# A two-layer decoder step on one core: last down panels kept on chip, first panels of the next head loaded earlier, ScalarE's splits ahead of its squares, one boundary's squares summed by TensorE

## The chip, the cores and the metric

The kernel runs on one NeuronCore of one Trainium2 chip. The metric is the time of one execution on the device in microseconds (us). Engines are called TensorE (PE, with PEld for its weight loads), VectorE (DVE), ScalarE (ACT), GpSimd (POOL) and SyncE (SP, whose queue of transfers is SPq).

## What is computed

One step of a hybrid decoder with two layers over 1056 columns (a prompt of 1024 tokens and 8 x 4 sample tokens), model width 1024, FFN width 2816, everything in float32 accuracy. Layer 0 mixes a short convolution with differential attention, layer 1 is an mLSTM with four heads. Each sub-layer stands between two norms:

```python
h = h + rmsnorm(mix, g[1])
h = h + rmsnorm(swiglu(rmsnorm(h, g[2]), w_gu[layer], w_down[layer]), g[3])
# swiglu: (silu(x @ gate) * (x @ up)) @ w_down
```

## The kernel before

All activations lie transposed on chip: 128 partitions by (feature tile, 1056 columns), and the columns are worked on in three thirds of 352. A matrix product in near float32 accuracy is made of three float16 matmuls: weight and activation are each split in a high part and a low part, and high x high, high x low and low x high are accumulated. A weight panel is 128 output features by all input tiles (8 tiles for most, KF = 11 for w_down). It is called a *visit*. SyncE loads it raw to one of two buffers (`w_raw[:, v % 2]`, `load_tile`), and only when the low split of visit v-2 is done. ScalarE makes the high part (`split_hi`, L242), VectorE the low part (`split_lo`, L255), in one of three slots of `w_split`, or in a named row of `arena` (`home`). `split_at` says at which *unit* both engines make the split of a visit: at the first unit after the last one that used the same slot (or later, by `late`). A unit is one panel times one third: 8 x 3 = 24 or 11 x 3 = 33 matmuls at L282 into one of six PSUM banks, then an evacuation.

The order on every engine is written out by hand, as the generators that `woven` and `steps` interleave. Each engine runs its list strictly in order, and so a wait holds back all that is behind it.

A *boundary* is the end of a sub-layer: for each third g, eight units whose result y goes to `ybuf` (a *pass*, `PASS[b][g]`), then the chain of norms for this third, which is woven into the eight units of the next one:

- the sum of y's squares: ScalarE squares each of the eight tiles (`act_square`, L530), GpSimd adds them up (`pool_sums`, L538 and L541), TensorE multiplies by ones (`pe_sum`, L506) after unit 0 of the next third;
- the first root (ScalarE L552, L555, VectorE L580, L581), then h += y scaled, in four pairs of tiles (VectorE L597, L601);
- the squares of h (ScalarE L562), which TensorE adds up itself: eight matmuls with 32 columns of ones each (`pe_part_sums`, L516, after unit 3), a copy by ScalarE (L565, semaphore `part_made`) and a last matmul with ones (`pe_whole_sum`, L523, in the middle of unit 4);
- the second root and the new activation u, high and low (VectorE L613 and L586, ScalarE L571).

Boundary 0 is the end of layer 0's mixer (w_out, eight resident panels), boundary 1 the end of its FFN, boundary 2 the end of the mLSTM, whose passes are short (2 tiles, L699 adds the rest), boundary 3 the end of the second FFN and of the kernel. The FFN has two halves of 11 gate and 11 up panels. The first half's down product is made with each panel used for all three thirds; the second half's is the pass of boundary 1 or 3 (`add_last_down`), which goes third by third and so loads all eight panels three times. Among the loads of its last third in boundary 1 stand the first two panels of the mLSTM (`early_q`, columns of w_in1). After a boundary the next stage begins with twelve units of four panels, third by third (`WAVE`, `pe_wave`). In boundary 1 h is saved to memory by GpSimd's queue (`h_spill`), a third at a time.

## Time and profile before

| | us |
|---|---|
| runs, median (lowest to highest) | 2910.95 (2905.79 to 2916.68), 3 runs |
| profiled execution, its own time | 2908.74 |
| its span, first to last instruction | 2907.1 |
| TensorE, VectorE, ScalarE, GpSimd busy | 2766.8, 1106.4, 913.2, 246.0 |
| mean granted clock of TensorE | 0.983 |

An idle time in the profile stands ahead of an instruction, with the engine, tile and line that ended it. Matmuls overlap, so that one of 128x352 is shown with 313 ns while one starts about every 150 ns. A granted clock of 1 is 2.4 GHz, 0.5 is 1.2 GHz; for a stretch the mean is given.

### The profile page before, as it was taken

How to read it: one execution, taken by the hardware profiler on the slowest of the kernel's cores; microseconds unless marked ns; L12 is line 12 of the kernel's file. 1: busy time of each engine (PE TensorE's matmuls, PEld its weight loads, DVE VectorE, ACT ScalarE, POOL GpSimd, SP SyncE). 2: the span in 40 equal slices, each digit the busy share in tenths (PEclk: the TensorE clock that was granted, in tenths of full speed). 3: DMA queues.
4: the chain of work that ended last, by engine and by line, in shares of the span. 5: the costliest groups of instructions: out<-in, count | busy, mean ns of one | idle time of the engine just before them, and what ended most of it. 6: DMA issues, size and time to landing. Idle time of an engine off the chain costs nothing.

```text
span 2907.1 us, 46616 instructions
## 1 busy us (share of the span) xinstructions
PE 2766.8 (95%) x19289; PEld 1815.3 (62%) x19289; DVE 1106.4 (38%) x1880; ACT 913.2 (31%) x1703; POOL 246.0 (8%) x356
## 2 busy tenths in 40 slices
PE   6999899989999999999799999999979999999997
PEld 4666565656666666666467666667646666666665
DVE  4455542327322112225653434344473221122354
ACT  4444432225322112224333232324353221122232
POOL 3000013212000000001100001010220000000011
PEclk8999999999999999999999999999999999999998
DMA  5211269661112111124564323321401121111243
GB/s 193 76 59 39 71 209 331 232 215 37 36 45 60 51 44 44 51 62 120 115 84 59 66 55 69 59 71 58 150 1 47 48 62 48 43 45 52 65 140 110
DMA packets 297789, 248.60 MB, mean 86 GB/s; under 512 B 10900, under 2 KB 263162, under 8 KB 296940
## 3 DMA queue, kind: packets, MB, share of 16 engines
q1 hardware_dynamic: 278332, 172.53, 22.8%
q0 software_dynamic: 19248, 73.10, 7.2%
q8 instruction: 155, 2.54, 0.4%
q14 instruction: 54, 0.44, 0.0%
HBM read 218.77 MB, written 26.81 MB: 84 GB/s over the span
## 4 chain that ended last, share of the span: by engine, by line
PE 84%; DVE 7%; ACT 3%; issue 3%; DMA 2%; SPq 1%; POOL 0%; DVEq 0%; POOLq 0%; ACTq 0%
PE ps L282 68%; PE ps L1462 2%; DVE arena L597 1%; DMA w_raw<-in_w_in 1%; PE ps L1450 1%; DVE hT L601 1%; PE ps L1148 1%; PE ps L2028 1%; PE ps L2019 1%; PE ps L1227 1%; PE ps L1997 1%; DMA hT<-in_cache_v 1%; PE ps L1972 1%; PE ps L2011 1%; ACT w_split L242 1%
## 5 line engine op out<-in xcount | busy, mean ns | idle before, releaser
L282 PE MATMUL ps<-u,w_split 128*128 128x352 f16 x9936 | 1531.8, 314 | 11.4 <-DVE arena L1112 3.9
L282 PEld LDWEIGHTS ps<-u,w_split 128*128 128x128 f16 x9936 | 969.7, 98 | 533.6 <-issue 26.5
L282 PE MATMUL ps<-arena,w_split 128*128 128x352 f16 x3960 | 610.5, 315 | 9.3 <-DVE w_split L255 7.8
L255 DVE SCALAR_TENSOR_TENSOR w_split<-w_raw,w_split 128x1024 f16<-128x1024 f32 (+2 forms) x214 | 285.3, 1334 | 774.1 <-ACT w_split L242 773.7
L282 PEld LDWEIGHTS ps<-arena,w_split 128*128 128x128 f16 x3960 | 388.2, 98 | 226.8 <-issue 11.8
L242 ACT ACTIVATE w_split<-w_raw 128x1024 f16<-128x1024 f32 (+2 forms) x214 | 242.7, 1135 | 63.4 <-PE ps L282 45.8
L828 ACT ACTIVATE arena<-arena 128x352 f16<-128x352 f32 x132 | 65.6, 497 | 378.2 <-DVE arena L861 378.2
L834 ACT ACTIVATE arena<-ps 128x352 f32<-128x352 f32 x132 | 61.0, 462 | 316.0 <-PE ps L282 316.0
L861 DVE SCALAR_TENSOR_TENSOR arena<-ps,arena 128x352 f32<-128x352 f32 x132 | 69.2, 524 | 198.9 <-PE ps L282 197.9
L538 POOL TENSOR_TENSOR arena<-arena 128x352 f32<-128x352 f32 x12 | 13.0, 1084 | 1324.3 <-ACT arena L530 1314.4
L848 DVE TENSOR_TENSOR arena<-arena 128x352 f16<-128x352 f32 x132 | 69.3, 525 | 71.8 <-ACT arena L828 71.8
L530 ACT ACTIVATE arena<-arena 128x352 f32<-128x352 f32 x96 | 47.5, 496 | 148.9 <-DVE arena L663 141.6
L541 POOL TENSOR_TENSOR arena<-arena 128x352 f32<-128x352 f32 x72 | 73.3, 1019 | 231.4 <-ACT arena L530 230.1
L1841 ACT ACTIVATE arena<-ps 128x352 f32<-128x352 f32 x66 | 30.5, 463 | 193.2 <-PE ps L282 193.2
L836 ACT ACTIVATE arena<-ps 128x352 f32<-128x352 f32 x48 | 22.2, 463 | 193.9 <-PE ps L282 193.9
L282 PE MATMUL ps<-u,arena 128*128 128x352 f16 x504 | 78.6, 316 | 1.9 <-ACT arena L834 1.3
L1462 PE MATMUL ps<-ident,hT 128*128 128x128 f32 x512 | 69.6, 279 | 2.2 <-issue 1.9
L1462 PEld LDWEIGHTS ps<-ident,hT 128*128 128x128 f32 x512 | 55.5, 140 | 25.4 <-issue 24.9
L282 PEld LDWEIGHTS ps<-u,arena 128*128 128x128 f16 x504 | 49.3, 99 | 32.0 <-issue 5.9
L1591 DVE COPY arena<-ps 128x512 f32<-128x512 f32 x64 | 44.2, 691 | 60.2 <-PE ps L1462 59.8
L1300 DVE TENSOR_REDUCE small<-ps 128x1 f32<-128x128 f32 (+7 forms) x64 | 45.5, 752 | 42.9 <-PE ps L1151 42.9
L1531 ACT ACTIVATE arena<-ps 128x512 f32<-128x512 f32 x64 | 38.2, 597 | 72.2 <-PE ps L1462 72.2
(357 smaller groups left out, 2198.2 us busy)
## 6 DMA issues: line engine op xcount, KB each, us to landing
w_raw<-in_w_gu SPq DMA_DIRECT2D x88, 512.0 KB, 3.8
w_raw<-in_w_down SPq DMA_DIRECT2D x64, 704.0 KB, 4.6
w_raw<-in_w_in SPq DMA_DIRECT2D x56, 512.0 KB, 6.7
hT<-in_cache_k SPq DMA_DIRECT2D x64, 256.0 KB, 4.0
hT<-in_cache_k POOLq DMA_DIRECT2D x64, 256.0 KB, 4.3
hT<-in_cache_v SPq DMA_DIRECT2D x64, 256.0 KB, 4.9
hT<-in_cache_v POOLq DMA_DIRECT2D x64, 256.0 KB, 5.5
hT<-in_state_C POOLq DMA_DIRECT2D x32, 256.0 KB, 4.1
```

The costliest lines, as they stand in the source:

```text
L242: act.activation(split_of(v, 0)[:, 0:kt * n], w_raw[:, v % 2, 0:kt * n], ACT.Copy, scale=WS).then_inc(w_hi, 1)
L255: dve.scalar_tensor_tensor(split_of(v, 1)[:, 0:kt * n], w_raw[:, v % 2, 0:kt * n], WS, split_of(v, 0)[:, 0:kt * n], ALU.mult, ALU.subtract ...
L282: ins = pe.matmul(ps[0:m, bank, 0:GW], split_of(v, wp)[:, k * w + col * P:k * w + col * P + m], x[:, xp, k0 + k, cols(g)], start=(k == 0 a ...
L530: act.activation(sq_y[k % 2], ybuf[:, k, cols(gg % 3)], ACT.Square).then_inc(sq_ready, 1)
L541: pool.tensor_tensor(sum_y, sum_y, sq_y[k % 2], ALU.add).then_inc(y_added, 1)
L828: act.activation(hid[:, 0, i, cols(g)], hidf[:, cols(g)], ACT.Copy).then_inc(hid_hi, 1)
L834: act.activation(gate[:, cols(g)], ps[:, bank, 0:GW], ACT.Silu, scale=1 / WS).then_inc(evac["act"], 1)
L848: dve.tensor_tensor(hid[:, 1, i, c], hidf[:, c], hid[:, 0, i, c], ALU.subtract).then_inc(hid_ready, 1)
L861: dve.scalar_tensor_tensor(hidf[:, cols(g)], ps[:, UNITS[n].bank, 0:GW], 1 / WS, gate[:, cols(g)], ALU.mult, ALU.mult).then_inc(evac["dve" ...
L1300: dve.tensor_reduce(neg_mx[:, n % 4:n % 4 + 1], score_cols(i, c)[:, 0:(i + 1) * P], AX.X, ALU.max, negate=True).then_inc(nm_ready, 1)
L1462: ins = pe.transpose(ps[:, 4 + e, h * P:(h + 1) * P], ring[:, f % RING, h * P:(h + 1) * P], ident[:, :])
L1591: dve.tensor_copy(kt[n % 2][:, :, P:2 * P], ps[:, 5, :].rearrange("p (h e) -> p h e", h=HEADS)).then_inc(kp_ev[1], 1)
```

## The change

- In the last down passes (boundaries 1 and 3) panel 4, in boundary 3 panel 6 too, is loaded and split once, to `arena` rows 21 and 22 (26 and 27), and used by all three thirds. Rows 21 and 22 are the FFN's `hidf` and `gate`, so ScalarE waits there for the last up unit.
- The two first mLSTM panels are loaded in the second half of layer 0's FFN, after panels 4 and 7.
- In the passes ScalarE makes the high split that is due at unit n+1 already in the step of unit n, ahead of its wait for the drained unit and of the square. VectorE's order of low splits is as before.
- In boundary 0 the sums of h's squares come a unit later (`SUM_AT`), and the chain's steps are moved with them (`PASS_ACT[0]`, `PASS_DVE[0]`).
- In boundary 2 the squares of y go to eight places (`y_sq`), TensorE adds them up as it does those of h, ScalarE copies the result (`part_made`), `pe_sum` follows. GpSimd has no part in it. ScalarE's and VectorE's orders are rewritten; the first FFN panel's split is due at unit 0 of the last third, and no step of the FFN's wave comes before the end of the third chain's second root on ScalarE.

```diff
@@ split_of
+            if VISITS[v].kt == KF:
+                return rows(home, 2).rearrange("p a t -> p (a t)").bitcast(F16)[:, part_ * KF * P:(part_ + 1) * KF * P]
@@ splits_hi
-            for v in split_at.get(n, ()):
+            for v in hi_at.pop(n, ()):
                 split_hi(act, v)
@@ add_ffn(layer, b, wave, early=())
+                    if half_ and i in (4, 7):
+                        for add in early[i == 7:][:1]:
+                            add()
@@ add_last_down
-                    v = add_visit(p_cols(w_down[layer, KF * P:2 * KF * P, :], i), KF, ("last", layer, g, i))
-                    PASS[b][g].append(add_unit(v, "dve", g))
-                    if g == 2 and i in (5, 6):
-                        early(i - 5)
+                    if i not in stays:
+                        v = add_visit(p_cols(w_down[layer, KF * P:2 * KF * P, :], i), KF, ("last", layer, g, i),
+                                      home=kept.get(i))
+                        if i in kept:
+                            stays[i] = v
+                    PASS[b][g].append(add_unit(stays.get(i, v), "dve", g))
...
+        add_last_down(0, 1, {4: 21})
...
-        late[wave[0] + 1] = WAVE[2][8]
-        add_last_down(1, 3, lambda j: None)
+        late[wave[0]], late[wave[0] + 1] = PASS[2][2][0], WAVE[2][8]
+        add_last_down(1, 3, {4: 21, 6: 26})
...
+        hi_at = dict(split_at)
@@ pe_sum, pe_part_sums, act_square, act_chain (boundary 2)
+            if (0, gg) in PART_TURN:
+                pe.wait_ge(part_made, PART_TURN[0, gg] + 1)
...
-                ins = pe.matmul(ps[q:q + 32, 7, 0:GW], ones[:, 0:32], ybuf[:, k, cols(gg % 3)], start=(k < 4),
-                                stop=(k >= 4))
+                ins = pe.matmul(ps[q:q + 32, 6 + a, 0:GW], ones[:, 0:32], ybuf[:, k, cols(gg % 3)] if a else y_sq[k],
+                                start=(k < 4), stop=(k >= 4))
...
+            if b == 2:
+                act.wait_ge(h_part, PART_TURN[0, gg] + 1)
+                act.wait_ge(y_summed, gg)
+                act.activation(sum_y, ps[:, 6, 0:GW], ACT.Copy, scale=1 / 32).then_inc(part_made, 1)
+                yield
@@ orders of the passes
-        PASS_ACT = (2, 2, 1, 2, 1, 1, 1, 1)
-        PASS_DVE = (3, 2, 0, 0, 2, 1, 1, 1)
+        PASS_ACT = ((2, 2, 1, 0, 1, 2, 2, 1), (2, 2, 1, 2, 1, 1, 1, 1))
+        PASS_DVE = ((3, 2, 0, 0, 0, 2, 2, 1), (3, 2, 0, 0, 2, 1, 1, 1))
+        SUM_AT = (4, 3)
@@ act_last_units
+                if b % 2 and (g, i) == (0, 0):
+                    act.wait_ge(hid_ready, up_turn[up_unit[b // 2, 1, KF - 1, 2]] + 1)
+                splits_hi(act, n + 1)
                 drained(act, n)
                 act_square(act, 3 * b + g, i)
@@ pe_short_passes
-                    if (g, i) == (1, 1):
+                    if (g, i) == (1, 0):
+                        pe_part_sums(pe, 6, 0)
+                    if (g, i) == (1, 2):
                         pe_sum(pe, 6)
                     if (g, i) == (2, 0):
+                        pe_part_sums(pe, 7, 0)
+                    if (g, i) == (2, 1):
                         pe_sum(pe, 7)
-                    if (g, i) == (2, 1):
+                    if (g, i) == (2, 2):
                         pe_part_sums(pe, 6)
-                    if (g, i) == (2, 2):
+                    if (g, i) == (2, 4):
                         pe_whole_sum(pe, 6)
+            pe_part_sums(pe, 8, 0)
             pe_sum(pe, 8)
```

The end of ScalarE's order in boundary 2 (a, b, c are the chains of the three thirds; a chain's steps are now copy, first root, four squares, copy, second root, four of u):

```diff
             steps(units_[2], 2)
             steps(a, 2)
             steps(b, 2)
-            steps(c, 1)
+            steps(c, 2)
             steps(b, 2)
             steps(c, 2)
             steps(b, 4)
-            steps(wave, 4)
             steps(c, 4)
-            woven(wave, c, (1,) * 4 + (0,) * 4)
+            woven(wave, c, (1,) * 4 + (0,) * 8)
```

## Rows read from the trace of the kernel before

**Rows 1.** the page, busy time and share of the span, TensorE

```profile
PE 2766.8 (95%) x19289; PEld 1815.3 (62%) x19289; DVE 1106.4 (38%) x1880; ACT 913.2 (31%) x1703; POOL 246.0 (8%) x356
```

**Rows 2.** waits of TensorE over the whole span: total, times, longest

```profile
PE ps L506 <- POOL arena L541: 12.9, 5, 5.6
```

**Rows 3.** stages: length; PE, PEld, DVE, ACT, POOL busy; PE clock; DMA share; GB/s

```profile
1350.00:1510.00 160.00, 136.68 (x873) 83.39 (x871) 94.85 (x124) 63.32 (x88) 19.48 (x18) 0.95 0.53 106
1453.00:1460.40 7.40, 7.30 (x34) 4.01 (x35) 5.42 (x11) 2.72 (x5) 3.13 (x2) 0.68 0.84 87
2095.00:2205.00 110.00, 91.94 (x551) 53.95 (x549) 75.99 (x109) 56.67 (x100) 22.07 (x21) 0.94 0.07 21
```

**Rows 4.** timeline, boundary 1, last third: start, duration, what, idle before

```profile
1419.98 0.37 SPq L216 DMA_DIRECT2D w_raw<-in_w_in  x1
...
1429.27 1.06 ACT L242 ACTIVATE arena<-w_raw 128x1024 f16<-128x1024 f32 x1 [6.40 <-DMA w_raw<-in_w_in]
...
1432.95 1.54 PE L523 MATMUL ps<-arena,ones 128*128 128x352 f32 x2 [8.17 <-ACT arena L565]
...
1434.28 14.15 PE L282 MATMUL ps<-arena,w_split 128*128 128x352 f16 x84
...
1453.10 7.34 PE L282 MATMUL ps<-arena,w_split 128*128 128x352 f16 x33 [4.67 <-DVE w_split L255]
...
1466.29 0.83 PE L506 MATMUL ps<-arena,ones 128*128 128x352 f32 x2 [2.16 <-POOL arena L541]
```

**Rows 5.** timeline, boundary 1, second third

```profile
1369.23 1.63 DVE L255 SCALAR_TENSOR_TENSOR w_split<-w_raw,w_split 128x1408 f16<-128x1408 f32 x1 [0.16 <-ACT w_split L242]
...
1372.55 0.79 PE L516 MATMUL ps<-arena,ones 128*32 128x352 f32 x4 [2.02 <-ACT arena L562]
...
1376.79 0.86 PE L523 MATMUL ps<-arena,ones 128*128 128x352 f32 x2 [1.11 <-ACT arena L565]
```

**Rows 6.** DMA issues, KB each, us to landing: whole span; last row 1515 to 1700

```profile
w_raw<-in_w_gu SPq DMA_DIRECT2D x88, 512.0 KB, 3.8
w_raw<-in_w_down SPq DMA_DIRECT2D x64, 704.0 KB, 4.6
...
w_raw<-in_w_in SPq DMA_DIRECT2D x12, 512.0 KB, 7.0
```

**Rows 7.** timeline, boundary 0, last third

```profile
698.69 0.79 PE L516 MATMUL ps<-arena,ones 128*32 128x352 f32 x4 [1.72 <-ACT arena L562]
...
701.21 0.76 PE L523 MATMUL ps<-arena,ones 128*128 128x352 f32 x2
...
705.22 1.06 ACT L242 ACTIVATE w_split<-w_raw 128x1024 f16<-128x1024 f32 x1 [1.11 <-DMA w_raw<-in_w_gu]
```

**Rows 8.** timeline, boundary 2, sums, squares and chains

```profile
2126.70 1.39 PE L516 MATMUL ps<-arena,ones 128*32 128x352 f32 x16
...
2133.94 0.52 DVE L580 SCALAR_TENSOR_TENSOR arena<-ps,arena 128x352 f32<-128x352 f32 x1
...
2143.43 1.51 PE L506 MATMUL ps<-arena,ones 128*128 128x352 f32 x2 [5.56 <-POOL arena L541]
...
2145.82 0.58 DVE L597 SCALAR_TENSOR_TENSOR arena<-arena,gains 128x352 f32<-128x352 f32 x1
...
2149.90 0.79 ACT L562 ACTIVATE arena<-hT 128x704 f32<-128x704 f32 x1 [1.25 <-DVE hT L601]
...
2156.97 0.52 DVE L580 SCALAR_TENSOR_TENSOR arena<-ps,arena 128x352 f32<-128x352 f32 x1
...
2163.92 1.83 DVE L586 TENSOR_TENSOR u<-arena,u 128x704 f16<-128x704 f32 x2
...
2173.29 2.07 PE L516 MATMUL ps<-arena,ones 128*32 128x352 f32 x8 [5.68 <-ACT arena L562]
...
2179.22 1.28 ACT L552 ACT_TABLE_LOAD   x1 [3.36 <-PE ps L523]
```

**Rows 9.** timeline, boundary 3, second third

```profile
2813.82 10.02 PE L282 MATMUL ps<-arena,w_split 128*128 128x352 f16 x66 [1.57 <-DVE w_split L255]
```

More of the change, by code:

```diff
@@ L334, in add_ffn_visit, with add_ffn @@
                              home=home)
-        def add_ffn(layer, b, wave):
+        def add_ffn(layer, b, wave, early=()):
             WAVE[b] = [add_ffn_unit(v, g) for g in range(3) for v in wave]
@@ L350, in add_ffn, with add_last_down @@
                             add_ffn_unit(v, g)
-        def add_last_down(layer, b, early):
-            PASS[b] = []
+        def add_last_down(layer, b, kept):
+            PASS[b], stays = [], {}
             for g in range(3):
@@ L384, in build @@
         FFU[0], FFU[1] = [], []
-        add_ffn(0, 0, wave)
         early_q = []
-        add_last_down(0, 1, lambda j: early_q.append(add_visit(in_col(0, j), KD, ("qkvo", 0, j), home=26 + j)))
+        add_ffn(0, 0, wave, [lambda j=j: early_q.append(add_visit(in_col(0, j), KD, ("qkvo", 0, j), home=26 + j))
+                             for j in range(2)])
+        add_last_down(0, 1, {4: 21})
         GATES = add_visit(w_cols(w_in1[0], slice(4 * D, 4 * D + 2 * HEADS)), KD, ("gates",), n=2 * HEADS)
@@ L497, in build @@
         NORMS = (((0, 1), (0, 2)), ((0, 3), (1, 0)), ((1, 1), (1, 2)), ((1, 3),))
+        PART_TURN = {(1, gg): gg for gg in range(6)}
+        PART_TURN.update({(0, 6): 6, (0, 7): 7, (1, 6): 8, (0, 8): 9, (1, 7): 10, (1, 8): 11})
+        y_sq = [third((10, 21, 22)[j // 3], j % 3) for j in range(KD)]
         def pe_sum(pe, gg):
@@ L563, in act_chain @@
                 yield
-            act.wait_ge(h_part, gg + 1)
+            act.wait_ge(h_part, PART_TURN[1, gg] + 1)
             act.activation(part_h, ps[:, 7, 0:GW], ACT.Copy, scale=1 / 32).then_inc(part_made, 1)
@@ L674, in pe_passes @@
                         pe.wait_ge(os_lo, 2)
-                    if g and i == 4 and b < 3:
+                    if g and b < 3 and i == SUM_AT[b] + 1:
                         half_ = VISITS[UNITS[n].visit].kt // 2
@@ L685, in pe_passes @@
                         pe_sum(pe, 3 * b + g - 1)
-                    if g and i == 3 and b < 3:
+                    if g and b < 3 and i == SUM_AT[b]:
                         pe_part_sums(pe, 3 * b + g - 1)
@@ L732, in act_boundary @@
             for g in (1, 2):
-                woven(act_last_units(act, b, g), act_chain(act, b, g - 1), PASS_ACT)
+                woven(act_last_units(act, b, g), act_chain(act, b, g - 1), PASS_ACT[b])
             tail = act_chain(act, b, 2)
@@ L752, in act_short_boundary @@
             steps(units_[0], 8)
-            steps(units_[1], 2)
+            steps(units_[1], 1)
+            steps(a, 1)
+            steps(units_[1], 1)
             steps(a, 1)
@@ L757, in act_short_boundary @@
             steps(units_[1], 2)
+            steps(b, 2)
             steps(a, 2)
-            steps(b, 1)
+            steps(units_[2], 3)
+            steps(a, 1)
             steps(units_[2], 2)
-            steps(a, 1)
-            steps(units_[2], 1)
             steps(a, 1)
@@ L765, in act_short_boundary @@
             steps(units_[2], 1)
-            steps(a, 1)
-            steps(units_[2], 2)
-            steps(a, 1)
+            steps(a, 2)
             steps(units_[2], 2)
@@ L793, in dve_short_boundary @@
             steps(b, 5)
-            steps(c, 2)
-            steps(wave, 4)
-            steps(c, 2)
-            woven(wave, c, (1, 1, 0, 1) + (0,) * 4)
+            steps(c, 4)
+            woven(wave, c, (1, 1, 0, 1) + (0,) * 8)
         def pool_boundary(pool, b):
```

26 lines of the change are left out of this document (17 added, 9 removed).

## The prediction

> **What bounds the kernel now.** I read the page first: TensorE is busy for 95% of the span [rows 1], so only its waits, and stretches in which it runs at the lower clock, can be won. The list of its waits comes next: the costliest is not for a panel but for a norm's sum, L506, which waits for GpSimd's adds, 12.9 us in 5 waits [rows 2]; L523, the sum behind ScalarE's copy part_made, is one of 8.17 us [rows 4]. The table by stage says where they lie: of 160 us around boundary 1 TensorE is idle for 23.3 (160.00 less 136.68), of 110 us around boundary 2 for 18.1, at a mean granted clock of 0.95 and 0.94 [rows 3]. So the change is worth what happens in the four boundaries, and the timeline of each has to be walked, engine by engine, in issue order.
>
> **Boundary 1, what goes.** In the last third two w_in panels stand among the w_down panels in SyncE's queue. The first is issued at 1419.98 and ScalarE's copy of it starts at 1429.27, after 6.4 us of waiting; behind that copy in ScalarE's queue stands part_made, and TensorE waits 8.17 us for it (L523). The second makes it wait 4.67 more for a panel. The late squares cost 2.16 at L506 [rows 4]. That is 15.0 us idle. After both stalls the clock is at 1.2 GHz for a while: L523 takes 1.54 us where it took 0.86 in the second third, the 84 matmuls behind it 14.15 where 84 x 0.15 are 12.6, and 33 matmuls 7.34 where they need 4.9 (0.15 each from [rows 9]; granted clock 0.68 in that stretch [rows 3]): 0.7 + 1.5 + 2.4 = 4.6 us. The change takes both w_in loads out of the passes and one w_down load out of each later third, so SyncE has 7 loads per later third of eight units of 4.9 us, not 8 to 10.
>
> **Boundary 1, what comes.** ScalarE now splits for unit i+1 before the square of unit i, and that split can wait for a load. A load is issued when VectorE's low split of two visits before has ended, and lands 4.6 us later [rows 6]. In the second third VectorE does that low split only after its chain, 1369.23 to 1370.9 [rows 5]; I walk it to 1371.4, because the split ahead delays the root by about 0.5. The load for the seventh panel then lands at 1376.1, its copy (1.06 x 1408/1024 = 1.4) ends at 1377.5, the square and part_made follow to 1378.4: TensorE's wait at L523 grows from 1.11 to 2.3, that at L516 from 2.02 to 2.4, and the one panel wait before it by 0.4. The last third has the same order, so instead of 8.17 it waits 2.2 there, and at L516 1.6. All idle that I walk for this stage after the change is 9.9 of the 23.3, so 13.4 goes, with 4.6 of clock: **18 us won**. Bounds: 20 if ScalarE never waits for a load (then the two L523 waits stay at 1.1), 12 if spill stores slow the loads to 7 us and each of the two waits brings a low clock as the 4.67 did.
>
> **The early panels in the FFN.** Two loads of 512 KB, two copies of 1.06 and two low splits of 1.2 (1.63 x 1024/1408). They lie beside matmuls: a visit there is 72 matmuls, 10.7 us, and TensorE has six banks of 24 matmuls (3.6 us) each, so ScalarE may be some 10 us late before it matters. In a stage with free queues such a load took 7.0 us [rows 6]; it is issued one visit ahead. Cost 0; without cover it would be 2 x 7.
>
> **Boundary 0.** TensorE loses 1.72 there at L516 and then reaches L523 at 701.21 without waiting [rows 7]. Moving the sums one unit later removes the 1.72. But the splits for unit 4 are two, wave[3] and the next gate panel, and they now stand in ScalarE's queue ahead of the square of unit 3, and part_made comes after unit 4. wave[3] can be loaded only after the low split of wave[1], which stands behind VectorE's fourth pair of h; with the root 1 us later (the split of wave[0] now precedes it) I walk that to 699.8. The two loads land at 703.8 and 705.3 (3.8 us [rows 6], 4.3 when they overlap), the second copy ends at 706.4, two squares and an evacuation at 707.8, part_made at 708.3. TensorE is there at 702.4. Before, the same copy also waited for its load, 1.11 at 705.22 [rows 7], but with part_made and the root already done. So a new wait of 5.9 us, and, as behind 4.67 in boundary 1, about 2 of lower clock. From 708.3, 60 matmuls remain where 84 remained at 701.21: 7.1 - 3.6 + 2.2 = **5.7 lost**. Lower bound of the loss: -1.7 if the loads are there in time; upper 7.
> The Trainium skill (DMA: Bandwidth & Descriptors, Anatomy of one DMA) fits a transfer as 2.0 us plus bytes over 436 GB/s: 3.2 us for 512 KB and 3.7 for 704 KB. The rows have 3.8, 4.6 and 7.0, so they decide; by the fit the wait here would be about 1 us shorter and those in boundary 1 about 0.9 each, 3 us in all.
>
> **Boundary 2.** GpSimd's adds go. TensorE gets three more groups of eight ones-matmuls; one takes 1.39 [rows 8], so they are 4 us of its work. In the first two thirds L506's shorter waits go, and pay for most of them. Third sum: it stood at 2143.43 after 5.56 us [rows 8]. Now it needs a copy by ScalarE, which in the new order stands behind squares 4 and 6 of the second third's h. VectorE makes that h after the first third's root and u, and the moved low split of wave[0]. First root 2133.94; root and u take 8.8 us when GpSimd is idle (2156.97 to 2165.75; 11.9 before with its adds beside them); split 1.2; two pairs of h up to the start of the last square 4.1 (2145.82 to 2149.90, the square of which row is the last); square and copy 1.3: the sum starts at 2149.3 [rows 8]. TensorE, done at 2137.9 before and now, with the part sums and the last square, at about 2140, idles 9 us, and wave unit 0 starts 6 us later. Given back later: the square for L516 no longer waits behind four FFN steps of ScalarE, so its 5.68 shrink to about 1 (-4.7), with the lower clock behind it (2.07 us for 8 matmuls where 16 took 1.39; -2.4), and ScalarE's table reload of 1.28 before the third root goes; one bank wait of 0.9 comes. 6.0 - 4.7 - 2.4 - 1.3 + 0.9 = **1.5 won**. Ends: 6 won (if VectorE, free of GpSimd, is 2 us faster in both chains), 5 lost (if what is given back is only the 4.7 and the long idle costs 3 of clock more).
>
> **Boundary 3.** With panels 4 and 6 kept, the wait of 1.57 for panel 4 [rows 9] goes, and a shorter one like it in the last third; the first root comes 0.5 later. The tail's transposes wait for ScalarE as before. **1.4 won**, between 0 and 3.
>
> **Sum.** -18 + 5.7 - 1.5 - 1.4 = -15.2 us, of which the copies that wait for loads are the disputed part. Against the profiled execution, 2908.7, that gives 2893.5; this execution is 2.2 below the median of the runs shown. I say **2893**.
>
> **Rivals.**
> A, the splits ahead do not wait: loads land in time in boundaries 0 and 1. For it: in the steady part of a pass there are 2 us of slack per load. Against: VectorE's low splits behind its chains. Boundary 0 turns into -1.7 and boundary 1 into -20: 2884.
> B, the blocked third sum of boundary 2 is not given back: +5 instead of -1.5: 2900. For it: nine idle microseconds are certain by the queue order. Against: the later wait of 5.68 is behind the same queue.
> C, boundary 1 wins only 12, because the spill stores (one starts at each third's end) meet the loads: 2899.
> D, slower, one mechanism: the loads become the bound of the passes. A raw buffer is busy for a copy, a low split and a load, 1.4 + 1.6 + 4.6 = 7.6 us, per two units of 4.9. With loads of 7 us, as w_in has, that is 10.0 and the point is passed; at 9 us it is 12.0, and each of the 40 loads costs 1.1 more: 2937. The kept panels speak against it, and rows of w_down at 4.6 do.
> E, the change does not act: early loads hold up the FFN by as much as they did the pass: 2907.
>
> **Chances.** Forecast 0.48, A 0.20, B 0.12, C 0.12, D 0.04, E 0.04. The forecast's own range is 2888 to 2898; with A and B and C held, 2883 to 2902. A difference of 0.5% (14.5 us) is about what a measurement of this kernel can tell from none. The line is at 2894.2: of the forecast's 0.48 some 0.34 lie below it, all of A, a little of B and C: faster 0.57; same 0.38 (the rest of them, and E); slower 0.05 (D, and what I may have missed).
>
> **What the changed profile would show.** Boundary 1: no w_in load among the w_down loads, L523's waits near 2 us each, no clock below 1 where the two stalls were, third sum of the stage some 18 us earlier. Boundary 0: an idle stretch of 4 to 7 us before the second L523, ended by ScalarE L565, with ScalarE's copies waiting for w_gu loads. Boundary 2: one long idle stretch of about 9 us before the third L506, released by ScalarE, no GpSimd adds, the later L516 wait near 1. Wrong would be: L523 in boundary 0 without a wait, waits of TensorE inside the first FFN's second half, or the time before wave unit 9 of boundary 2 more than 4 us off.

## The result, and the profile after

The changed kernel takes 2892.38 us (median of 5 runs, 2891.65 to 2895.77); the kernel before takes 2911.65 us (5 runs beside it, 2905.79 to 2916.68). The ratio is 0.9939, with a 95% interval of 0.9925 to 0.9953. The prediction was 2893.0 us. The profiled execution took 2892.26 us, its span is 2890.3 us. The page's line of busy time, which answers to [rows 1]:

```profile
PE 2764.8 (96%) x19337; PEld 1815.1 (63%) x19337; DVE 1088.2 (38%) x1874; ACT 904.3 (31%) x1698; POOL 246.1 (9%) x335
```

TensorE is busy for 2.0 us less and the span is 16.8 us shorter, so nearly all that went was waiting. The list of TensorE's waits, which answers to [rows 2] (total, times, longest). L540 is the whole sum (before, L523), L521 the sum of y (L506), L533 the part sums (L516), L582 and L593 ScalarE's scaled copies (L582 of y's part sums, new in boundary 2; L593 of h's, before L565), L590 the squares of h (L562), L244 and L257 the high and low split (L242 and L255):

```profile
PE ps L540 <- ACT arena L593: 10.7, 3, 6.4
PE ps L521 <- ACT arena L582: 8.6, 1, 8.6
...
PE ps L533 <- ACT arena L590: 4.4, 3, 1.9
```

No wait for GpSimd's adds is left; the two costliest waits of a boundary are now for ScalarE. To see where the time came from I cut both traces at the same instructions: from the first to the third sum of y in boundaries 0, 1 and 3, and from the first unit of the pass to the last whole sum in boundary 2. The windows of the kernel before, then of the changed one (length; PE, PEld, DVE, ACT, POOL busy; PE clock; DMA share; GB/s):

```profile
651.99:717.91 65.92, 64.12 (x426) 39.75 (x425) 45.76 (x61) 35.96 (x63) 15.04 (x14) 1.00 0.14 41
1353.43:1466.29 112.86, 90.09 (x562) 54.12 (x560) 70.65 (x89) 46.01 (x60) 17.18 (x16) 0.92 0.55 109
2099.00:2178.37 79.37, 64.10 (x367) 36.27 (x368) 58.84 (x82) 42.78 (x79) 22.07 (x21) 0.91 0.03 7
2796.58:2887.26 90.68, 81.34 (x542) 53.62 (x540) 47.56 (x57) 32.46 (x39) 13.51 (x14) 0.98 0.39 119
```

```profile
650.20:721.13 70.93, 64.54 (x426) 39.97 (x425) 44.21 (x60) 35.54 (x63) 14.87 (x14) 0.95 0.13 38
...
1356.73:1451.80 95.07, 86.68 (x562) 53.26 (x560) 66.91 (x86) 41.37 (x56) 21.21 (x16) 0.98 0.46 102
2084.54:2162.82 78.28, 67.81 (x415) 37.71 (x416) 49.14 (x79) 41.46 (x77) 0.00 (x0) 0.93 0.03 8
...
2780.21:2870.39 90.18, 81.98 (x541) 53.81 (x540) 41.22 (x53) 27.51 (x35) 18.46 (x14) 0.98 0.28 87
```

Boundary 0 is 5.0 us longer, boundary 1 17.8 shorter, boundary 2 1.1 shorter, boundary 3 0.5 shorter. The rest of the 16.8 is 1.8 ahead of boundary 0, where the change does nothing, and 0.8 in the second FFN; the first FFN with the two early panels keeps its length (635.60 after 635.52), and so does the mLSTM stage.

In boundary 1 TensorE's idle time (the length less its busy time) fell from 22.8 to 8.4 us, and its busy time by 3.4.

The same stages for every kernel of this study, in us, one profiled execution each, cut at the same instructions of each one's timeline, with the median of its runs and of the runs of the kernel before on the same chip:

| kernel | b. 0 | b. 1 | mLSTM | b. 2 | b. 3 | median | before there | ratio (95%) |
|---|---|---|---|---|---|---|---|---|
| before | 65.92 | 112.86 | 632.71 | 79.37 | 90.68 | 2911.65 | | |
| changed | 70.93 | 95.07 | 632.74 | 78.28 | 90.18 | 2892.38 | 2911.65 | 0.9939 (0.9925 to 0.9953) |
| before + early panels only | 65.92 | 97.17 | 632.72 | 78.57 | 92.44 | 2893.91 | 2908.16 | 0.9950 (0.9937 to 0.9963) |
| before + splits ahead only | 75.52 | 117.15 | 632.76 | 79.12 | 95.46 | 2925.25 | 2908.16 | 1.0055 (1.0041 to 1.0069) |
| changed, b. 0 not ahead | 69.56 | 94.83 | 631.07 | 77.53 | 90.18 | 2890.80 | 2908.16 | 0.9941 (0.9927 to 0.9954) |
| changed, copy first in b. 2 | 70.72 | 96.46 | 629.39 | 72.25 | 88.51 | 2885.69 | 2908.16 | 0.9925 (0.9912 to 0.9938) |
| changed, b. 0 as before | 65.92 | 96.44 | 632.75 | 77.77 | 90.18 | 2891.09 | 2909.28 | 0.9934 (0.9921 to 0.9948) |
| the last two together | 65.92 | 93.59 | 632.78 | 73.05 | 88.51 | 2881.89 | 2909.28 | 0.9905 (0.9890 to 0.9921) |
| changed, nothing kept | 70.77 | 96.51 | 629.39 | 77.57 | 94.06 | 2894.14 | 2909.28 | 0.9949 (0.9936 to 0.9963) |
| changed, never ahead | 70.22 | 91.18 | 631.10 | 77.88 | 89.41 | 2885.73 | 2909.28 | 0.9926 (0.9913 to 0.9940) |
| all mended | 65.92 | 91.18 | 631.06 | 72.66 | 89.46 | 2876.72 | 2910.16 | 0.9889 (0.9874 to 0.9904) |
| all mended, nothing kept | 65.92 | 97.16 | 634.40 | 72.65 | 89.96 | 2885.78 | 2910.16 | 0.9922 (0.9908 to 0.9936) |

Stages with the same code show how far one such length can be trusted. Boundary 1 is the same in the changed kernel and in the four that only mend boundary 0, boundary 2 or both: it took 93.59 to 96.46 us there, and boundary 3 took 88.51 to 90.18. Boundary 0 took 69.56 and 70.22 us in the two kernels that have its moved steps and no split ahead in it. TensorE's idle time scatters less (6.9 to 8.4 us in that boundary 1, 8.20 or 8.21 in that boundary 3), and most of the rest is clock. So small differences are read below by idle time, not by length.

In boundary 0 the timeline of the changed kernel shows what blocks the sum (start, duration, what, idle before):

```profile
700.71 1.06 ACT L244 ACTIVATE arena<-w_raw 128x1024 f16<-128x1024 f32 x1 [3.51 <-DMA w_raw<-in_w_gu]
703.65 1.06 ACT L244 ACTIVATE w_split<-w_raw 128x1024 f16<-128x1024 f32 x1 [1.88 <-DMA w_raw<-in_w_gu]
...
705.88 0.45 ACT L593 ACTIVATE arena<-ps 128x352 f32<-128x352 f32 x1
...
706.37 1.54 PE L540 MATMUL ps<-arena,ones 128*128 128x352 f32 x2 [6.37 <-ACT arena L593]
```

ScalarE stands in front of two w_gu panels, 3.51 and 1.88 us, and the scaled copy that the whole sum waits for comes only behind both. In boundary 1 the same happens on a smaller scale, where [rows 4] had 8.17 and 4.67:

```profile
1379.72 1.38 ACT L244 ACTIVATE w_split<-w_raw 128x1408 f16<-128x1408 f32 x1 [3.40 <-DMA w_raw<-in_w_down]
...
1381.89 1.54 PE L540 MATMUL ps<-arena,ones 128*128 128x352 f32 x2 [2.38 <-ACT arena L593]
...
1429.87 0.86 PE L540 MATMUL ps<-arena,ones 128*128 128x352 f32 x2 [1.97 <-ACT arena L593]
```

In boundary 2, where [rows 8] had 5.56 for GpSimd and later 5.68 for ScalarE:

```profile
2124.64 1.66 PE L533 MATMUL ps<-arena,ones 128*32 128x352 f32 x4 [0.70 <-ACT arena L547]
...
2128.39 1.22 DVE L257 SCALAR_TENSOR_TENSOR w_split<-w_raw,w_split 128x1024 f16<-128x1024 f32 x1
...
2131.56 0.79 ACT L590 ACTIVATE arena<-hT 128x704 f32<-128x704 f32 x1 [4.01 <-DVE hT L629]
2133.60 0.79 ACT L590 ACTIVATE arena<-hT 128x704 f32<-128x704 f32 x1 [1.25 <-DVE hT L629]
2134.30 0.45 ACT L582 ACTIVATE arena<-ps 128x352 f32<-128x352 f32 x1
...
2134.89 1.51 PE L521 MATMUL ps<-arena,ones 128*128 128x352 f32 x2 [8.58 <-ACT arena L582]
...
2160.30 0.79 PE L533 MATMUL ps<-arena,ones 128*32 128x352 f32 x4 [1.09 <-ACT arena L590]
```

The copy L582 is ready to go once the part sums have ended at 2126.30 (2124.64 plus 1.66), but it stands behind two squares that wait for VectorE until 2134.30. The experiments ask for each part what it is worth alone, and for each of these two blocked copies what put it there.

### The profile page after: what moved, and what is told of

It is laid out like the page before. It is cut to its first block, busy times and chain, and to the rows that moved or that the text cites. A ratio compares the mean times of both kernels' runs of the same rounds, so it can differ in the third digit from the quotient of the medians.

```text
span 2890.3 us, 46645 instructions
## 1 busy us (share of the span) xinstructions
PE 2764.8 (96%) x19337; PEld 1815.1 (63%) x19337; DVE 1088.2 (38%) x1874; ACT 904.3 (31%) x1698; POOL 246.1 (9%) x335
## 4 chain that ended last, share of the span: by engine, by line
PE 89%; DVE 4%; ACT 2%; DMA 2%; issue 2%; SPq 1%; POOL 0%; DVEq 0%; ACTq 0%; POOLq 0%
PE ps L284 72%; PE ps L1496 2%; PE ps L1484 1%; PE ps L1182 1%; PE ps L2062 1%; PE ps L2053 1%; PE ps L1261 1%; PE ps L2031 1%; PE ps L2006 1%; DMA hT<-in_cache_v 1%; PE ps L2045 1%; DVE arena L625 1%; PE ps L1535 1%; DVE hT L629 1%; PE ps L2019 1%
## 5 line engine op out<-in xcount | busy, mean ns | idle before, releaser
L284 PE MATMUL ps<-arena,w_split 128*128 128x352 f16 x3663 | 562.4, 314 | 3.0 <-DVE w_split L257 1.5
L257 DVE SCALAR_TENSOR_TENSOR w_split<-w_raw,w_split 128x1024 f16<-128x1024 f32 (+2 forms) x205 | 272.8, 1332 | 732.2 <-ACT w_split L244 731.8
L284 PEld LDWEIGHTS ps<-arena,w_split 128*128 128x128 f16 x3663 | 358.0, 98 | 201.4 <-issue 10.9
L244 ACT ACTIVATE w_split<-w_raw 128x1024 f16<-128x1024 f32 (+2 forms) x205 | 230.8, 1127 | 150.7 <-PE ps L284 99.1
L284 PE MATMUL ps<-arena 128*128 128x352 f16 x657 | 102.7, 316 | 0.0
L882 DVE TENSOR_TENSOR arena<-arena 128x352 f16<-128x352 f32 x132 | 69.3, 525 | 72.3 <-ACT arena L862 72.3
L564 POOL TENSOR_TENSOR arena<-arena 128x352 f32<-128x352 f32 x54 | 73.8, 1367 | 176.5 <-ACT arena L552 176.2
L284 PEld LDWEIGHTS ps<-arena 128*128 128x128 f16 x657 | 64.7, 99 | 38.1 <-issue 2.9
```

Source lines behind the costliest of these rows:

```text
L244: act.activation(split_of(v, 0)[:, 0:kt * n], w_raw[:, v % 2, 0:kt * n], ACT.Copy, scale=WS).then_inc(w_hi, 1)
L257: dve.scalar_tensor_tensor(split_of(v, 1)[:, 0:kt * n], w_raw[:, v % 2, 0:kt * n], WS, split_of(v, 0)[:, 0:kt * n], ALU.mult, ALU.subtract ...
L284: ins = pe.matmul(ps[0:m, bank, 0:GW], split_of(v, wp)[:, k * w + col * P:k * w + col * P + m], x[:, xp, k0 + k, cols(g)], start=(k == 0 a ...
L564: pool.tensor_tensor(sum_y, sum_y, sq_y[k % 2], ALU.add).then_inc(y_added, 1)
L882: dve.tensor_tensor(hid[:, 1, i, c], hidf[:, c], hid[:, 0, i, c], ALU.subtract).then_inc(hid_ready, 1)
```

## The experiments

### One part alone: the early panels

The kernel before, with the two w_in panels placed in the FFN and nothing else.

```diff
-        def add_ffn(layer, b, wave):
+        def add_ffn(layer, b, wave, early=()):
...
+                    if half_ and i in (4, 7):
+                        for add in early[i == 7:][:1]:
+                            add()
...
-                    if g == 2 and i in (5, 6):
-                        early(i - 5)
...
```

> The kernel before with one part of the change alone: the two early w_in panels (homes 26 and 27) are placed inside the first FFN's second half. Nothing else changes. Theory A (the late w_in panel alone sets boundary 1): the stage between the first third's whole sum and the third's PE sum loses the 14.15 us wait and the cold clock behind it; the third's sum of boundary 1 comes 15 to 18 us earlier, all other stages keep their length within 0.5 us, and the run takes 2892 to 2896 us of about 2909. Rival B (the panels were only one of two limits, and the w_down panels that the full change keeps are needed for the rest): boundary 1 gains 9 us or less, because the next panel's transfer ends the wait instead, and the run takes 2900 us or more. Rival C (the loads collide with the FFN's own): the first FFN grows by over 1 us.

Measured: 2893.91 us. Its windows of boundary 1 and boundary 3:

```profile
1352.11:1449.28 97.17, 86.94 (x561) 53.02 (x560) 68.95 (x87) 43.89 (x58) 16.39 (x16) 0.98 0.48 115
...
2778.77:2871.21 92.44, 82.33 (x541) 53.86 (x540) 47.44 (x57) 32.57 (x39) 13.48 (x14) 0.97 0.38 117
```

Boundary 1 falls by 15.7 us, at the low end of theory A, and B and C fall: the first FFN takes 635.52 us as before, so the early loads, copies and low splits are hidden whole. The expectation misnames one thing: the 14.15 us of [rows 4] are the run of 84 matmuls behind the wait, and the wait itself was 8.17. This part alone gives a ratio of 0.9950, where the full change gives 0.9939. What is left in boundary 1, beside waits for ScalarE of 1.1 to 2.0 us that the kernel before has too, are a wait of 1.24 us for a split panel and two for GpSimd's adds, 1.28 and 2.47. Two stages left the 0.5 us that A allowed: boundary 2 is 0.8 shorter, and boundary 3 came out 1.8 longer; its two waits for panels are those of the kernel before (1.57, and 0.28 for 0.29), 1.0 us of the difference is TensorE's busy time for the same matmuls, 0.8 an issue gap in front of the transposes (2.90, elsewhere 2.10).

### One part alone: the splits ahead

The kernel before, with the high splits of unit n + 1 ahead of the square of unit n.

```diff
-            for v in split_at.get(n, ()):
+            for v in hi_at.pop(n, ()):
...
+        hi_at = dict(split_at)
...
+                splits_hi(act, n + 1)
                 drained(act, n)
                 act_square(act, 3 * b + g, i)
```

> The kernel before with one part alone: ScalarE makes the high splits of the next unit ahead of the square of this one, at all four boundaries. Panels and sums as before. Theory A (the splits ahead queue ScalarE behind w_gu panels that land late in boundary 0, and everything behind them slips): boundary 0 grows by 4 to 7 us, with a wait of a whole sum on the scaled copy of ScalarE of about 6 us in it; the other boundaries shorten by 0 to 2 us; the run takes 2911 to 2916 us where the kernel before takes about 2909. Rival B (the growth of boundary 0 comes from the new order of the units with the later sum, not from the splits): boundary 0 keeps its length within 1 us and the run takes 2907 to 2910 us.

Measured: 2925.25 us, slower than the kernel before by 0.41 to 0.69%. Windows of its boundaries 0 and 1:

```profile
650.63:726.15 75.52, 68.74 (x427) 41.17 (x425) 45.61 (x61) 35.73 (x63) 14.96 (x14) 0.93 0.13 36
1361.67:1478.82 117.15, 92.10 (x562) 55.05 (x560) 71.47 (x89) 45.52 (x60) 20.20 (x16) 0.88 0.53 105
```

In boundary 0 A's mechanism holds and its size was too small; for the other boundaries A was wrong, since it had them 0 to 2 us shorter, and the run came out 9 us above its range. Boundary 0 grows by 9.6 us (waits of TensorE for ScalarE of 0.67, 1.68 and 4.35, and 4.6 us more of busy time at a mean clock of 0.93), boundary 1 by 4.3, boundary 3 by 4.8, and boundary 2 alone is 0.3 shorter. In boundary 1 the timeline shows ScalarE in front of the late w_in panels, with the squares of h behind the first and the scaled copy behind the second. TensorE waits 11.81 us for those squares and 8.54 for that copy, where the kernel before waits 8.17 for the copy and 4.67 for a panel:

```profile
1437.72 1.06 ACT L242 ACTIVATE arena<-w_raw 128x1024 f16<-128x1024 f32 x1 [9.25 <-DMA w_raw<-in_w_in]
...
1439.07 0.77 ACT L563 ACTIVATE arena<-hT 128x704 f32<-128x704 f32 x1
...
1439.89 1.39 PE L517 MATMUL ps<-arena,ones 128*32 128x352 f32 x4 [11.81 <-ACT arena L563]
...
1452.49 1.06 ACT L242 ACTIVATE arena<-w_raw 128x1024 f16<-128x1024 f32 x1 [11.32 <-DMA w_raw<-in_w_in]
...
1453.84 0.44 ACT L566 ACTIVATE arena<-ps 128x352 f32<-128x352 f32 x1
```

### Boundary 0: the splits back behind the squares

```diff
-                splits_hi(act, n + 1)
+                if b:
+                    splits_hi(act, n + 1)
```

> The changed kernel with the splits ahead of the squares at boundaries 1 to 3 only; at boundary 0 a split is issued after the square, as before. Theory A (in boundary 0 ScalarE stands in front of a split whose w_gu panel has not landed, and the whole sum waits 6.4 us behind it, then runs at the lower clock): boundary 0 gives back 4 to 6 us, the 6.4 us wait is gone, and the run takes 2886 to 2888 us of 2892. Rival B (the wait comes from the panels themselves and moves to the matmul of the next unit): boundary 0 keeps its length within 1 us, a wait of TensorE for the split of the late panel takes the place, and the run takes 2891 to 2893 us.

Measured: 2890.80 us. Both theories miss: boundary 0 gives back 1.4 of its 5.0 us, and the wait that stays is still one for the scaled copy (4.98 us), not one for a panel:

```profile
701.77 1.06 ACT L244 ACTIVATE arena<-w_raw 128x1024 f16<-128x1024 f32 x1 [2.22 <-DMA w_raw<-in_w_gu]
704.35 1.06 ACT L244 ACTIVATE w_split<-w_raw 128x1024 f16<-128x1024 f32 x1 [1.52 <-DMA w_raw<-in_w_gu]
...
706.19 0.45 ACT L593 ACTIVATE arena<-ps 128x352 f32<-128x352 f32 x1
```

The square of unit 3 now runs ahead of the two splits, but the copy L593 still comes behind them. The diff says why: PASS_ACT, PASS_DVE and SUM_AT of boundary 0 also moved the sums and the chain by one unit, and that unit is the one whose panels are late. So a third cause had to be tried. (The run without any split ahead, further below, has the same code in this boundary and took 70.22 us, with 5.54 at the copy; so what the splits ahead cost here, beside the moved steps, is 0.7 to 1.4 us.)

### Boundary 0 in the order of the kernel before

```diff
+                if b:
+                    splits_hi(act, n + 1)
...
-        PASS_ACT = ((2, 2, 1, 0, 1, 2, 2, 1), (2, 2, 1, 2, 1, 1, 1, 1))
-        PASS_DVE = ((3, 2, 0, 0, 0, 2, 2, 1), (3, 2, 0, 0, 2, 1, 1, 1))
-        SUM_AT = (4, 3)
+        PASS_ACT = ((2, 2, 1, 2, 1, 1, 1, 1), (2, 2, 1, 2, 1, 1, 1, 1))
+        PASS_DVE = ((3, 2, 0, 0, 2, 1, 1, 1), (3, 2, 0, 0, 2, 1, 1, 1))
+        SUM_AT = (3, 3)
```

> The changed kernel with boundary 0 in the order of the kernel before: no splits ahead of the squares there, and the part sums and the chain's steps one unit earlier again (PASS_ACT, PASS_DVE and SUM_AT of boundary 0 as those of boundary 1). The run with the splits alone taken out left 3.6 of boundary 0's 5.0 us, with a wait of 5.0 us for the scaled copy, which ScalarE now issues behind two splits of w_gu panels that land late. Theory A (the moved steps carry that copy behind the late panels): boundary 0, from the first sum to the third, falls from 70.9 to 65.9 us as in the kernel before, the copy's wait goes, and the run takes 2886.5 to 2889 us of 2892. Rival B (something else that the change brings, such as the home of the kept panel or the transfers' order, holds boundary 0): it stays above 68 us and the run takes 2890 us or more.

Measured: boundary 0 takes 65.92 us, to the hundredth what it takes in the kernel before, and the wait for the copy is gone. Theory A holds for the stage. The run did not come out as it said: 2891.09 us (2887.12 to 2892.10), where 2886.5 to 2889 was expected. The profile shows 3.7 us more ahead of boundary 0 and 1.4 more in boundary 1, where this edit does nothing, and in both it is TensorE's busy time that is longer and not its idle time:

```profile
0.00:653.93 653.93, 581.37 (x5093) 388.42 (x5094) 275.85 (x521) 242.39 (x531) 106.81 (x194) 0.96 0.47 158
...
1355.37:1451.81 96.44, 88.45 (x561) 53.82 (x560) 66.89 (x86) 41.36 (x56) 21.23 (x16) 0.96 0.45 101
```

So 5 us won in one stage are not shown by this run's median alone; the two runs below that hold boundary 0 as before do show them.

### Boundary 2: the scaled copy ahead of two squares

```diff
             steps(a, 2)
+            steps(c, 1)
             steps(b, 2)
-            steps(c, 2)
+            steps(c, 1)
             steps(b, 2)
             steps(c, 2)
```

> The changed kernel with one step of ScalarE's order at boundary 2 moved: the scaled copy that the third third's sum waits for is issued ahead of the second third's last two squares of h, not behind them. Theory A (the sum's 8.58 us wait is ScalarE's order, the copy being late behind squares that wait for VectorE): the third's sum comes 5 to 8 us earlier, the cold clock behind it shrinks, and boundary 2 shortens by 3 to 6 us, so that the run takes 2886 to 2889 us. Rival B (the last third's own chain of root, h, squares and sums on VectorE sets the end of the stage, and the wait of TensorE is idle time that nothing stands behind): the wait falls by 5 us or more but boundary 2 keeps its length within 1 us and the run takes 2891 to 2893 us.

Measured: 2885.69 us, boundary 2 72.25 us for 78.28. The copy now goes 1.2 us after the part sums' end, and the wait shrinks from 8.58 to 1.74:

```profile
2124.16 1.66 PE L533 MATMUL ps<-arena,ones 128*32 128x352 f32 x4 [0.69 <-ACT arena L547]
...
2126.97 0.44 ACT L582 ACTIVATE arena<-ps 128x352 f32<-128x352 f32 x1
...
2127.56 1.51 PE L521 MATMUL ps<-arena,ones 128*128 128x352 f32 x2 [1.74 <-ACT arena L582]
```

This is theory A, at or just over its upper end: the long wait was ScalarE's order, and of the 6.8 us that went from it 6.0 reach the end of the stage. Rival B, a chain of VectorE that sets the end anyway, falls.

### Both mended places

The edits of the last two together.

> Both mended places together: boundary 0 as in the kernel before, and at boundary 2 the scaled copy ahead of the second third's last two squares (that alone took the run to 2885.7 us). Theory A (the two stages are apart and their gains add): boundary 0 gives back 5 us and boundary 2 6 us, and the run takes 2880 to 2883 us. Rival B (the time given back ahead of the mLSTM stage is lost in its waits for transfers): the stage between boundary 1 and boundary 2 grows by what boundary 0 gives back, and the run takes 2885 us or more.

Measured: 2881.89 us, inside theory A's range; 65.92 and 73.05 us in the two stages, and the mLSTM stage at 632.78 against 632.74. The gains add, and nothing between takes them back.

### Nothing kept

The changed kernel, with each third loading all eight last down panels.

```diff
-        add_last_down(0, 1, {4: 21})
+        add_last_down(0, 1, {})
...
-        add_last_down(1, 3, {4: 21, 6: 26})
+        add_last_down(1, 3, {})
```

> The changed kernel with no down panel kept: every third loads all eight again, at both last down projections. Early w_in panels, orders and sums as in the changed kernel. Theory A (with the early panels out of the pass, the w_down transfers of 4.6 us run under units that take some 5 us each, so that what is kept was hidden anyway): boundaries 1 and 3 keep their length within 1 us each, and the run takes 2891 to 2894 us. Rival B (the ring of raw buffers is behind at the boundaries and a kept panel relieves it): TensorE waits for splits of w_down panels in boundaries 1 and 3, 1 to 3 us in each, and the run takes 2895 to 2898 us.

Measured: 2894.14 us, at the upper end of theory A, but the stages say otherwise. Boundary 1 is 1.4 longer with no more idle time (8.1 us, where the changed kernel has 8.4), so that is clock:

```profile
1357.39:1453.90 96.51, 88.40 (x561) 53.86 (x559) 69.06 (x87) 43.63 (x58) 20.79 (x16) 0.96 0.49 116
```

Boundary 3 is 3.9 longer, with idle time of 11.6 us for 8.2: waits for split panels of 0.74, 1.57 and 1.04 where the changed kernel has the 0.74 alone, and an issue gap of 2.87 for 2.10. The mLSTM stage was 3.3 shorter in this execution and hides most of it in the span (1.9 longer). So A holds for boundary 1 and B for boundary 3, as long as the splits go ahead.

### Never ahead

The changed kernel, without the line `splits_hi(act, n + 1)`.

> The changed kernel with ScalarE's splits behind the square of the unit at every boundary, as in the kernel before; all else as changed. Theory A (with all panels landed in time the place of a split is worth only the waits of the part sums and whole sums on ScalarE, 1 to 2 us a boundary): boundary 0 gives 1.4 us back as in the run without them there, boundary 1 grows by 0.5 to 1.5 us, boundary 3 by 0 to 1.5 us, and the run takes 2891 to 2894 us. Rival B (the splits ahead carry the gain at boundary 1, since a split behind the square holds the next unit): boundary 1 grows by 3 us or more and the run takes 2895 us or more.

Measured: 2885.73 us. Both theories expected the splits ahead to be worth something at boundaries 1 and 3, and both fall. The kernel without them is 6.6 us faster by the medians, but those were taken beside different runs of the kernel before, and the intervals of the two ratios overlap (0.9913 to 0.9940, and 0.9925 to 0.9953); so the stages have to show it. TensorE's idle time is shorter by 0.8 us in boundary 0, 2.3 in boundary 1 and 0.7 in boundary 3, and 0.5 longer in boundary 2. Its window of boundary 1, and the waits for the copy in it:

```profile
1356.95:1448.13 91.18, 85.09 (x561) 52.65 (x559) 67.22 (x86) 41.26 (x56) 17.11 (x16) 1.00 0.48 108
```

```profile
1380.31 0.86 PE L540 MATMUL ps<-arena,ones 128*128 128x352 f32 x2 [1.11 <-ACT arena L593]
...
1426.20 0.86 PE L540 MATMUL ps<-arena,ones 128*128 128x352 f32 x2 [1.11 <-ACT arena L593]
```

The waits at L540 are 1.11 and 1.11 where the changed kernel has 2.38 and 1.97, and the wait of 0.74 for a panel is gone. Of the 3.9 us, 2.3 are idle time (8.4 less 6.1) and 1.6 TensorE's busy time: the mean clock is 1.00 for 0.98.

### All mended, and what is kept in it

The changed kernel, never ahead, boundary 0 in the old order, the copy first in boundary 2; then the same with nothing kept.

> The changed kernel with no split ahead of a square at any boundary, boundary 0 in the order of the kernel before, and at boundary 2 the scaled copy ahead of the last two squares of the second third; early w_in panels, kept down panels and the y-sums of boundary 2 on TensorE stay. Theory A (the splits ahead cost 3.9 us at boundary 1 and 0.8 at boundary 3, the moved steps 3.6 to 5.0 at boundary 0, the late copy 6.0 at boundary 2, each in its own stage): stages of 65.9, 91.2, 72 to 73 and 88.5 to 89.5 us, and the run takes 2874 to 2879 us. Rival B (the shorter boundary 1 of the run without splits ahead was luck of the clock): boundary 1 stays at 93.5 us or more, and the run takes 2880 us or more.

> The kernel of the run before this, with no down panel kept. Theory A (the kept panels save the waits on splits of w_down panels: 1.57 and 0.29 us at boundary 3, 1.24 at boundary 1, and the lower clock that follows them): boundary 1 takes 93 to 95 us instead of 91.2, boundary 3 90.5 to 92.5 instead of 88.5 to 89.5, and the run is 3 to 6 us slower than the one with kept panels. Rival B (a kept panel matters only where a split ahead puts ScalarE in front of a late one, which is gone here): both boundaries keep their length within 1 us and the run is less than 2 us slower.

Measured, all mended: 2876.72 us (2875.46 to 2879.57), a ratio of 0.9889 (0.9874 to 0.9904), whose interval lies wholly below that of the change. Theory A holds for each stage (boundary 0 takes 65.92 us again):

```profile
1354.13:1445.31 91.18, 85.09 (x561) 52.65 (x559) 67.21 (x86) 41.26 (x56) 17.09 (x16) 1.00 0.47 108
...
2076.37:2149.03 72.66, 67.17 (x415) 36.89 (x416) 49.14 (x79) 41.44 (x77) 0.00 (x0) 0.98 0.03 8
...
2766.42:2855.88 89.46, 81.99 (x542) 54.31 (x540) 41.33 (x53) 27.29 (x35) 13.52 (x14) 0.97 0.29 89
```

Without the kept panels: 2885.78 us, 9.1 more by the medians, where A expected 3 to 6 and B less than 2. A has the mechanism, but no size of it: boundary 1 came out above its 93 to 95 us, boundary 3 below its 90.5. Boundary 1 takes 97.16 for 91.18, all but 0.5 of it idle time, with three waits that the kernel with the kept panel doesn't have, one for a split panel and two at the sum of y for GpSimd's adds (L564):

```profile
1352.41:1449.57 97.16, 85.57 (x561) 52.55 (x560) 68.97 (x87) 43.89 (x58) 16.40 (x16) 1.00 0.48 115
```

```profile
1400.29 0.83 PE L521 MATMUL ps<-arena,ones 128*128 128x352 f32 x2 [1.29 <-POOL arena L564]
...
1412.20 5.10 PE L284 MATMUL ps<-arena,w_split 128*128 128x352 f16 x33 [1.24 <-DVE w_split L257]
...
1449.57 0.93 PE L521 MATMUL ps<-arena,ones 128*128 128x352 f32 x1 [2.70 <-POOL arena L564]
```

Boundary 3 is only 0.5 longer: the waits of 1.58 and 0.29 us are back (idle 9.3 for 7.5), and its busy time is 1.4 shorter. In the profile a further 3.3 lie in the mLSTM stage, whose instructions are the same; whether the medians hold that too is open.

Four of the kernels with early panels now hold every pair of kept or not kept and ahead or behind. TensorE's idle time in us, with the length of the stage behind it:

| | boundary 1, ahead | boundary 1, behind | boundary 3, ahead | boundary 3, behind |
|---|---|---|---|---|
| panels kept | 8.4 (95.07) | 6.1 (91.18) | 8.2 (90.18) | 7.5 (89.46) |
| nothing kept | 8.1 (96.51) | 11.6 (97.16) | 11.6 (94.06) | 9.3 (89.96) |

In boundary 1 the two parts remove the same waits. With nothing kept the splits ahead save 3.5 us of idle time, though the stage is only 0.7 shorter, because the clock takes most of it; with the panel kept they cost 2.3 (0.8 to 2.3 over the five executions of that code). In boundary 3 they cost idle time either way, 0.7 and 2.2, of which 0.8 is the issue gap.

## Why the prediction was right, point by point

**Boundary 1, 18 us won: 17.8.** I had 13.4 of idle time and 4.6 of clock; it was 14.4 of idle time and 3.4 of busy time. Taken in this order, the early panels alone take 112.86 to 97.17 (-15.7), the kept panel takes that to 91.18 (-6.0; the run with everything but the splits ahead), and the splits ahead take it back to 95.07 (+3.9): -17.8. Another order gives other sizes with the same end: with the splits ahead in place from the start (+4.3), the early panels are worth 20.6 us (117.15 to 96.51) and the kept panel 1.4, which is no idle time at all. The waits that I walked for the splits ahead, 2.3 and 2.2 at the whole sum and 2.4 and 1.6 at the part sums, were 2.38, 1.97, 1.91 and 1.39. I had named 20 as the bound if ScalarE never waits for a load; without the splits ahead it is 21.7 (16.7 of idle time and 5.0 of busy time, at a mean clock of 1.00).

**The early panels in the FFN, 0: 0.** 635.60 and, alone, 635.52 us, where the kernel before has 635.52.

**Boundary 0, 5.7 lost: 5.0.** The wait of 5.9 was 6.37, and the scaled copy ended 0.2 us from where I had it (706.33, with the stage begun 1.8 earlier than in the kernel before: 708.1 by its clock, for 708.3). The mis-sized term is the lower clock behind the wait, 2.2 us: the whole sum took 1.54 for 0.76 and the 60 matmuls 9.90, where 84 took 12.69, which is 1.6. The 1.72 did go. What the prediction did not see is that the step "moving the sums one unit later" changes its sign with the splits ahead. Each of the two edits puts the copy behind the same two late panels, so their costs don't add: the splits ahead alone cost 9.6 in the old order, the moved steps alone 3.6 (4.3 in a second kernel with the same code there), both together 5.0. The later sums win 4.6 where the splits go ahead and lose 3.6 to 4.3 where they don't.

**Boundary 2, 1.5 won: 1.1.** The third sum was to start at 2149.3 by the clock of the kernel before; with the pass begun 14.46 earlier (2084.54 for 2099.00), 2134.89 is 2149.35. The idle stretch of 9 us was 8.58, the later one "about 1" was 1.09 where 5.68 stood. The sum hides two parts: with the copy in its place the stage takes 72.3 to 73.1 us, so TensorE's sums in place of GpSimd's adds, with the orders rewritten around them (no run has the one without the other), are worth about 6 us against the 78.57 of the kernel with GpSimd's, and the late copy took some 5 to 6 of them back (6.0 in the run with that edit alone). I had called that wait certain by the queue order; the runs show that it was.

**Boundary 3, 1.4 won: 0.5.** The waits of 1.57 and 0.29 for panels went, as walked. The split ahead, which the sum for this stage left out, brings a wait of 0.74 for a panel: idle time fell by 1.1 us, and without the split ahead it falls by 1.9. The rest is clock: busy time grew by 0.6, with 66 matmuls at 11.69 us where [rows 9] has 10.02. By length the split's cost can't be seen here, since two kernels with the splits ahead took 88.51 us and the two without them 89.41 and 89.46.

**The rivals.** A, in which the splits ahead don't wait, fell in both places. B, C, D and E fell by boundary 2's, boundary 1's and the FFN's lengths; the point of D was not reached, but the loads had less slack than I gave them, since without the kept panel and with the splits behind the squares boundary 1 is 6.0 us longer.

**The sum, and some luck.** The sum was -15.2 us. The profiled executions differ by 16.5, and the medians by 19.3 (2911.65 to 2892.38). The 2893.0 comes nearer to 2892.38 than that, because the sum was laid against a profiled execution of 2908.7, which is 2.9 below the median measured beside the change; the sentence that names such a gap (2.2) does not add it. Laid against 2911.65 the sum gives 2896.4.

**The DMA fit.** The fit of a transfer that the prediction takes from the Trainium skill (DMA: Bandwidth & Descriptors, Anatomy of one DMA) is given in that section for transfers issued by GpSimd, and these loads are issued by SyncE. The sum goes by the 3.8 and 4.6 us of [rows 6] and does not need it.

**What the prediction did not ask.** The sum hides -15.7 for one part, and a part, the splits ahead, that costs idle time in boundaries 0, 1 and 3 of the changed kernel. It was forecast as "ScalarE's split can wait for a load", with the price, but never set against what it gives. By these runs that is 3.5 us of idle time in boundary 1 with nothing kept, and nothing once the panel is kept.

## What to carry to other kernels

On an engine with one queue in order, an instruction that can wait for a load belongs behind everything that another engine is waiting for; issuing it one unit early wins only if its load is there, and here, with the panels kept, it lost in boundaries 0, 1 and 3. When a change has four parts, walk each one's gain and loss by stage: a sum that comes out right can hold a part worth taking out, here the splits ahead, the moved steps and the late copy, worth 15.2 us by the stages and 15.7 by the medians. A part should also be tried with the others in and out: the kept panel was worth 1.4 us of boundary 1 with the splits ahead and 6.0 without them. A load that stood in the way at this boundary cost nothing in a stage with 72 matmuls for each panel; that alone was some four fifths of the gain.

## What was not expected of the hardware

The same instructions don't take the same time in every execution. The mLSTM stage, with 3896 or 3897 matmuls, took 629.39, 631.1, 632.7 or 634.40 us over these kernels, and TensorE's idle time in it was 3.5 us each time; the shortest (the copy first in boundary 2) and the longest (all mended, nothing kept):

```profile
1454.68:2084.07 629.39, 625.86 (x3896) 419.01 (x3896) 265.91 (x618) 217.03 (x464) 57.90 (x83) 1.00 0.36 75
```

```profile
1449.57:2083.97 634.40, 630.87 (x3896) 421.21 (x3896) 267.16 (x619) 217.08 (x464) 58.60 (x84) 0.99 0.35 74
```

What differs is busy time. Cut into slices of 10 us, the stage has a granted clock of 1.00 everywhere but in a few places, where a slice has 0.83 or two neighbours share the same loss; one of them, in the changed kernel (length; busy as above; PE clock; DMA share; GB/s):

```profile
1843.50:1853.54 10.04, 10.04 (x54) 6.63 (x53) 4.90 (x12) 3.42 (x7) 0.00 (x0) 0.83 0.48 36
```

TensorE is busy for the whole of that slice, so no wait inside it made the clock fall. A mean of 0.83 is a stretch at 1.2 GHz among 2.4. The twelve traces have one, two, three or four such places, and the length goes by their number: 629.39 us with one (two traces), 631.06 to 631.10 with two (three), 632.71 to 632.78 with three (six), 634.40 with four (one). Each costs 1.7 us. Why one execution has one and another four is open. The Trainium skill (TensorE: Matmul & The Clock Gate, Part 1) says of a kernel's start that the number of cold matmuls varies from run to run; these traces show the clock varying in the middle of a kernel too. It limits what one profiled execution can tell: a stage should be compared by its idle time first, and busy time that differs by 1.7 us or a multiple of it be looked for in the clock before anything else.

VectorE's two-input operations were slower beside GpSimd's adds: in boundary 2 two of them took 2.31 us in the kernel before, with four adds of GpSimd beside them, and 1.08 in the changed kernel, which has none there. The kernel before, VectorE and GpSimd:

```profile
2138.65 2.31 DVE L613 SCALAR_TENSOR_TENSOR arena<-hT,gains,arena 128x352 f32<-128x352 f32 x2
```

```profile
2137.92 5.36 POOL L541 TENSOR_TENSOR arena<-arena 128x352 f32<-128x352 f32 x4 [0.99 <-ACT arena L530]
```

The changed kernel:

```profile
2123.73 1.08 DVE L641 SCALAR_TENSOR_TENSOR arena<-hT,gains,arena 128x352 f32<-128x352 f32 x2
```

The Trainium skill (GPSIMD Engine Reference, Specifications) lists GpSimd's interface to SBUF as shared with VectorE, with contention for VectorE's instructions with two SBUF inputs; the rows agree. The chain of root and u took 8.8 us (2119.70 to 2128.47) where it took 11.9 before, as the prediction had it.
